# State-space scan by pairs of heads, and cross attention's small steps, placed between the chunks of weight units

## What is computed

```python
    xbc = jax.nn.silu(_depthwise_causal_conv(xbc, ssd_conv_w, ssd_conv_b))
    xs, bm, cm = jnp.split(xbc, [SSD_INNER, SSD_INNER + SSD_GROUPS * SSD_STATE], axis=-1)
...
    cb = jnp.einsum('bclgn,bcsgn->bgcls', Cc, Bc)
    y_diag = jnp.einsum('bgrcls,bcsgrp->bclgrp', cb[:, :, None] * Lmat, X)
    decay_states = jnp.exp(a_cs[..., -1:] - a_cs)
    states = jnp.einsum('bclgn,bgrcl,bclgrp->bcgrpn', Bc, decay_states, X)
...
    y_off = jnp.einsum('bclgn,bcgrpn,bgrcl->bclgrp', Cc, prev_states, jnp.exp(a_cs))
...
    y = (y + ssd_D.astype(jnp.float32)[:, None] * xh).astype(x.dtype).reshape(b, s, SSD_INNER)
    yg = (y * jax.nn.silu(z)).reshape(b, s, SSD_GROUPS, SSD_INNER // SSD_GROUPS)
    y = _rmsnorm(yg, ssd_norm_g.reshape(SSD_GROUPS, SSD_INNER // SSD_GROUPS), SUBLN_EPS)
    ssd_out = y.reshape(b, s, SSD_INNER) @ w_branch_ssd
    g_attn, g_ssd = jnp.split(jax.nn.sigmoid(gate_logits + b_gate), N_BRANCH, axis=-1)
    mixed = (g_attn * attn_out + g_ssd * ssd_out) @ w_mix_out
...
    sc = jnp.einsum('bqhd,bkhd->bhqk', qx, kx).astype(jnp.float32) * (XA_HEAD_DIM ** -0.5)
    p = jax.nn.softmax(sc, axis=-1).astype(vx.dtype)
```

## Time and profile before

| | |
|---|---|
| median of three runs | 2845.43 us |
| profiled execution | 2849.17 us, span in the trace 2847.1 us |
| PE busy | 2652.6 us, 93% |
| PE weight loads, beside the matmuls | 2131.6 us, 75% |
| DVE, ACT, POOL busy | 1302.4, 1068.2, 183.1 us |
| HBM read | 237.94 MB |
| scan stage, 40 units | from 1661.6 us |
| gated stage, 24 units | from 2026.8 us |
| next stage's first matmul | 2170.5 us |

### The profile page before, as it was taken

One profiled execution on the slowest core, in us unless ns is written; L12 is line 12 of the kernel. 1 busy time (PEld: TensorE's weight loads), 2 busy tenths in 40 slices (PEclk: granted clock), 3 DMA queues, 4 the chain that ended last, 5 costly groups with the idle time before them and its releaser, 6 DMA issues. The chain is left out here.

```text
span 2847.1 us, 33597 instructions
## 1 busy us (share of the span) xinstructions
PE 2652.6 (93%) x12052; PEld 2131.6 (75%) x12052; DVE 1302.4 (46%) x1758; ACT 1068.2 (38%) x1677; POOL 183.1 (6%) x114
## 2 busy tenths in 40 slices
PE   7998999999999999996999998889799799799997
PEld 5886777788888888884777776677587587588885
DVE  7544453454443344424344455666534533533333
ACT  5444453232222323323556434443423443332321
POOL 1000000010001000012000001101303200100000
PEclk9999999999999999998999999999899899899998
DMA  3212122233333333332222223222233122133332
GB/s 117 72 52 86 60 66 74 82 96 96 98 97 95 98 97 98 92 97 69 67 67 67 68 97 96 96 92 85 67 96 102 60 91 80 52 96 96 96 95 82
DMA packets 69471, 241.20 MB, mean 85 GB/s; under 512 B 7968, under 2 KB 8992, under 8 KB 69264
## 3 DMA queue, kind: packets, MB, share of 16 engines
q1 hardware_dynamic: 69392, 240.14, 26.7%
HBM read 237.94 MB, written 2.16 MB: 84 GB/s over the span
## 5 line engine op out<-in xcount | busy, mean ns | idle before, releaser
L193 PE MATMUL acc<-h_hi,w_hi 128*128 128x512 f32 x2128 | 856.3, 402 | 26.7 <-PEq L230 17.2
L166 DVE TENSOR_TENSOR w_lo<-w_raw,w_hi 128x1024 fp32r<-128x1024 f32 (+1 forms) x422 | 513.9, 1218 | 791.7 <-ACT w_hi L155 791.5
L155 ACT ACTIVATE w_hi<-w_raw 128x1024 fp32r<-128x1024 f32 (+1 forms) x422 | 441.5, 1046 | 1093.9 <-PE acc L195 1092.6
L194 PE MATMUL acc<-h_lo,w_hi 128*128 128x512 f32 x2128 | 833.9, 392 | 0.0
L195 PE MATMUL acc<-h_hi,w_lo 128*128 128x512 f32 x2128 | 833.5, 392 | 0.0
L193 PEld LDWEIGHTS acc<-h_hi,w_hi 128*128 128x128 f32 x2128 | 402.8, 189 | 129.4 <-issue 40.9
L194 PEld LDWEIGHTS acc<-h_lo,w_hi 128*128 128x128 f32 x2128 | 403.2, 189 | 86.7 <-issue 6.7
L195 PEld LDWEIGHTS acc<-h_hi,w_lo 128*128 128x128 f32 x2128 | 402.6, 189 | 85.6
L193 PE MATMUL acc<-6_hid_hi,w_hi 128*128 128x512 f32 x352 | 136.9, 389 | 0.0
L194 PE MATMUL acc<-6_hid_lo,w_hi 128*128 128x512 f32 x352 | 136.9, 389 | 0.0
L195 PE MATMUL acc<-6_hid_hi,w_lo 128*128 128x512 f32 x352 | 136.9, 389 | 0.0
(11 more groups left out here) (436 smaller groups left out, 3505.0 us busy)
## 6 DMA issues: line engine op xcount, KB each, us to landing
w_raw<-in_w_gu SPq DMA_DIRECT2D x132, 512.0 KB, 3.5
w_raw<-in_w_down SPq DMA_DIRECT2D x48, 512.0 KB, 3.5
w_raw<-in_w_ssd SPq DMA_DIRECT2D x40, 512.0 KB, 3.5
w_raw<-in_w_swa SPq DMA_DIRECT2D x28, 512.0 KB, 3.5
w_raw<-in_w_gla SPq DMA_DIRECT2D x24, 512.0 KB, 3.5
w_raw<-in_w_da SPq DMA_DIRECT2D x24, 512.0 KB, 3.5
w_raw<-in_w_ssd_out SPq DMA_DIRECT2D x24, 512.0 KB, 3.5
w_raw<-in_w_xa SPq DMA_DIRECT2D x24, 512.0 KB, 3.6
```

The source lines that it names most:

```text
L155: c.nc.scalar.activation(c.w_hi[:, k % 2, 0:chunks * P], c.raw[:, k % 2, 0:chunks * P], ACT.Copy).then_inc(c.hi_done, 1)
L166: c.nc.vector.tensor_tensor(c.w_lo[:, k % 2, 0:chunks * P], c.raw[:, k % 2, 0:chunks * P], c.w_hi[:, k % 2, 0:chunks * P].bitcast(F32), AL ...
L193: pe.matmul(out, hi, x_hi[:, j, 0:cols], start=first, stop=False)
L194: pe.matmul(out, hi, x_lo[:, j, 0:cols], start=False, stop=False)
```

## The change

The scan stage becomes `scan_stage` with one stream of 48 units, without a loop: for each group B, C, then x and z of each pair in turn, and after the last group the eight gate units that stood in the gated stage. Every small step of a pair is done for that pair alone and placed between two chunks of a later unit: x's transposes and the states in the next x unit, the sum of squares, `po` and `pd` in the next z unit. The tap with the newest input and the bias is taken by ACT from PSUM (`Identity`) instead of by DVE. The decays of a pair are weighed in one instruction of 1024 columns. The gated stage becomes `values_stage` with 16 units; the split of `y_ssd` now stands in front of its first unit. In cross attention a head's score tiles go, two at a time, behind chunks 3 and 7 of the next head's first unit, its transposes behind chunks 1 and 5 of the fourth, its outputs behind chunk 1 of the fifth.

The core of the diff (left out: declarations, DMA order, the parts of `ssd_stage` that are removed and stand above; lines of a new function are shown without what they replace):

```diff
+            def score(n):
+                if n == 0:
+                    wait_evacuated(c, pe, i, 6 * j - 2)
+                    wait_evacuated(c, pe, i, 6 * j - 1)
+                att.score_tile(pe, g - 1, n, lambda m: [(q[:, before, e, :], k_[:, before, e, :]) for e in range(2)])
+            def scores_between(chunk):
+                if chunk in (3, 7):
+                    for n in (chunk // 2 - 1, chunk // 2):
+                        score(n)
+            def turns_between(chunk):
+                if chunk in (1, 5):
+                    for n in (chunk // 2, chunk // 2 + 1):
+                        att.transpose_tile(pe, g - 1, before, n)
+            def outputs():
+                att.outputs(pe, g - 1, lambda kt, e: v_tok[:, before, kt, e * P:(e + 1) * P])
+            def outputs_between(chunk):
+                if chunk == 1:
+                    outputs()
...
+            if not project:
+                for n in range(NT):
+                    score(n)
+                pe.wait_ge(v_done, g + 1)
+                att.transposes(pe, g - 1, before)
+                outputs()
+                return
+            multiply_tile(c, pe, i, 6 * j, 6 * j, mem, MEM, between=scores_between if attend else None)
+            for u in (1, 2):
+                multiply_tile(c, pe, i, 6 * j + u, 6 * j + u, mem, MEM)
             if attend:
                 pe.wait_ge(v_done, g + 1)
+            multiply_tile(c, pe, i, 6 * j + 3, 6 * j + 3, mem, MEM, between=turns_between if attend else None)
+            multiply_tile(c, pe, i, 6 * j + 4, 6 * j + 4, h, norm=None if attend else norm,
+                          between=outputs_between if attend else None)
...
             g = 2 * i + j
+            if attend:
+                att.maxima(dve, g - 1, (j - 1) % 2)
             if project:
                 for u in range(2):
                     split_lo(c, dve, i, 6 * j + u)
             if attend:
                 weights(g - 1, (j - 1) % 2)
             if project:
-                for u in (2, 3):
+                for u in (2, 3, 4):
                     split_lo(c, dve, i, 6 * j + u)
             if attend:
                 finish(g - 1)
             if project:
-                split_lo(c, dve, i, 6 * j + 4)
-                att.maxima(dve, g, j % 2)
                 split_lo(c, dve, i, 6 * j + 5)
         heads_of(dve, head)
...
+def scan_units(a):
+    order = [(n, g) for g in range(SSD_GROUPS) for n in ("b", "c", *(f"{n}{j}" for j in range(GH // 2) for n in "xz"))]
+    index = {"b": 0, "c": 1, **{f"x{j}": 2 + j for j in range(4)}, **{f"z{j}": 6 + j for j in range(4)}}
+    units = [(KC, lambda i, n=n, g=g: a["w_ssd"][g, index[n]]) for n, g in order]
+    units += [(KC, lambda i, g=g: a["w_ssd_out"][g, 0]) for g in range(KC)]
...
+        def turn_x(p):
+            i, j = divmod(p, GP)
+            pe.wait_ge(silued, 6 * i + 3 + j)
+            if p > 0:
+                pe.wait_ge(x_dt, p)
             for t in range(NT):
+                mm = pe.transpose(px[:, at(t)], xs[:, j % 2, at(t)], c.ident[:])
+            mm.then_inc(turned, 1)
+        def make_states(p):
+            pe.wait_ge(x_end, p + 1)
+            if p > 0:
+                pe.wait_ge(states, 5 * p)
             for t in range(3):
+                mm = pe.matmul(pst[:, at(t)], b_tok[:, t, :], xend[:, t, :], start=True, stop=True)
+            mm.then_inc(state_raw, 1)
+        def outputs(p):
+            pe.wait_ge(states, 5 * (p + 1))
+            if p > 0:
+                pe.wait_ge(moved_done, p)
+                pe.wait_ge(skip_done, p)
+            for t in range(1, NT):
+                mm = pe.matmul(po[:, at(t)], state[:, t - 1, :], c_[:, at(t)], start=True, stop=True)
+            mm.then_inc(off_done, 1)
+            pe.wait_ge(weighed, p + 1)
+            for h in range(2):
+                for t in range(NT):
+                    mm = pe.matmul(pd[64 * h:64 * h + 64, at(t)], xdt[:, t, SSD_P * h:SSD_P * (h + 1)],
+                                   m[:, h, at(t)], start=True, stop=True)
+            mm.then_inc(diag_done, 1)
...
+        for i in range(G):
+            p = GP * i
+            if i == 0:
+                unit("b", i)
+                unit("c", i)
+                unit("x0", i, between({3: [(turn_b, i)]}))
+            else:
+                unit("b", i, between({0: [(turn_x, p - 1)], 6: [(make_states, p - 1)]}))
+                unit("c", i, between({5: [(mean_square, p - 2), (outputs, p - 1)]}))
+                unit("x0", i, between({3: [(turn_b, i)]}))
+            unit("z0", i, between({5: [(c_by_b, i)]}))
+            unit("x1", i, between({0: [(turn_x, p)], 6: [(make_states, p)]}))
+            unit("z1", i, between({5: [(mean_square, p - 1), (outputs, p)] if i > 0 else [(outputs, p)]}))
+            for j in range(2, GP):
+                unit(f"x{j}", i, between({0: [(turn_x, p + j - 1)], 6: [(make_states, p + j - 1)]}))
+                unit(f"z{j}", i, between({5: [(mean_square, p + j - 2), (outputs, p + j - 1)]}))
+        p = GP * G
+        unit("gate", 0, between({0: [(turn_x, p - 1)], 6: [(make_states, p - 1)]}))
+        unit("gate", 1, between({5: [(mean_square, p - 2), (outputs, p - 1)]}))
+        unit("gate", 2)
+        unit("gate", 3, between({0: [(mean_square, p - 1)]}))
+        for g in range(4, KC):
+            unit("gate", g)
...
+        def take(name, i):
+            n, k = CONV.index(name), places[name, i]
+            wait_tile(c, act, 0, k)
+            if 6 * i + n >= 2:
+                act.wait_ge(convolved, 6 * i + n - 1)
+            act.activation(u[:, n % 2, 3:], c.acc[k % 2][:], ACT.Copy).then_inc(taken, 1)
+            act.activation(conv[:, n % 2, :], c.acc[k % 2][:], ACT.Identity, scale=small("ssd_conv_w_2", 24 * i + 18 + n),
+                           bias=small("ssd_conv_b_2", 6 * i + n)).then_inc(c.acc_free[k % 2], 1)
+            split_hi(c, act, 0, k)
...
+        def z_silu(j, i):
+            k, p = places[f"z{j}", i], GP * i + j
+            wait_tile(c, act, 0, k)
+            if p >= 2:
+                act.wait_ge(y_done, p - 1)
+            act.activation(zs[:, j % 2, :], c.acc[k % 2][:], ACT.Silu).then_inc(c.acc_free[k % 2], 1)
+            wait_evacuated(c, act, 0, k)
+            act.sem_inc(z_done, 1)
+            split_hi(c, act, 0, k)
...
+        act.wait_ge(padded, 1)
+        for i in range(G):
+            act.preload_act_table(ACT.Silu)
+            take("b", i)
+            silu("b", i)
+            take("c", i)
+            silu("c", i)
+            act.wait_ge(b_turned, i + 1)
+            act.activation(b_tok[:], pb[:], ACT.Copy).then_inc(b_tok_done, 1)
+            if i > 0:
+                square(GP * i - 1)
             for j in range(GP):
+                act.preload_act_table(ACT.Silu)
+                take(f"x{j}", i)
+                silu(f"x{j}", i)
+                z_silu(j, i)
+                act.preload_act_table_set(EXP_LN_SET)
+                decays(GP * i + j)
+                if j > 0:
+                    square(GP * i + j - 1)
+                if j == 1 and i > 0:
+                    root(i - 1)
+        act.preload_act_table(ACT.Sigmoid)
+        gate(0)
+        gate(1)
+        square(GP * G - 1)
+        gate(2)
+        act.preload_act_table_set(EXP_LN_SET)
+        root(G - 1)
+        act.preload_act_table(ACT.Sigmoid)
+        for g in range(3, KC):
+            gate(g)
...
+        def scale_x(p):
+            i, j = divmod(p, GP)
+            dve.wait_ge(turned, p + 1)
+            if p > 0:
+                dve.wait_ge(diag_done, p)
+            dve.tensor_tensor(by_head(xdt[:]), by_head(px[:].rearrange("p (t l) -> p t l", t=NT)), rate(i, j, DT, NT),
+                              ALU.mult).then_inc(x_dt, 1)
+            dve.wait_ge(x_dt, p + 1)
+            if p > 0:
+                dve.wait_ge(state_raw, p)
+            dve.tensor_tensor(by_head(xend[:]), by_head(xdt[:, 0:3]), rate(i, j, TO_END, 3), ALU.mult).then_inc(x_end, 1)
...
+        def finish(p):
+            i, j = divmod(p, GP)
+            dve.wait_ge(off_done, p + 1)
+            dve.wait_ge(pair_decayed, p + 1)
+            if p > 0:
+                dve.wait_ge(joined, p)
+            dve.tensor_tensor(moved[:, P:], po[:, P:], pair_decay[:, P:], ALU.mult).then_inc(moved_done, 1)
+            dve.wait_ge(diag_done, p + 1)
+            dve.wait_ge(silued, 6 * i + 3 + j)
+            dve.scalar_tensor_tensor(y_out[:, p, :], xs[:, j % 2, :], small("ssd_D_2", p), pd[:],
+                                     ALU.mult, ALU.add).then_inc(skip_done, 1)
...
+        for i in range(G):
+            p = GP * i
+            low("b", i)
+            convolve("b", i)
+            if i > 0:
+                finish(p - 1)
+            low("c", i)
+            convolve("c", i)
             for j in range(GP):
+                low(f"x{j}", i)
+                convolve(f"x{j}", i)
+                cut(p + j)
+                if j > 0:
```

(54 more changed lines are left out.)

432 lines of the change are left out of this document (187 added, 245 removed).

## The result

| kernel | us, median | range of its runs | ratio to before | 95% interval |
|---|---|---|---|---|
| before | 2844.9 | 2843.5 to 2853.5 | 1 | |
| changed | 2795.8 | 2795.2 to 2800.9 | 0.9825 | 0.9802 to 0.9848 |

The changed kernel takes 49 us less, 1.75%. The forecast of 2804 us was right in sign and in range (2786 to 2826), and 8 us too high.

A forecast was written before the change was run, and what follows sets the result against it. TensorE (PE), busy 93% of the span, was taken as the bound, so gains must come from its idle or lower-clock time. Profiled 2849.17 - 36.6 - 4.5 = 2808 us, less 3.7 to the median: 2804 us, range 2786 to 2826.

The forecast's parts named there:

- head, group starts, port: Scan stage: half clock at its head 3.0 us, waits at four group starts 17, GpSimd and DVE sharing a port 6.
- PE's own work: Scan stage: small steps 5.0 us a pair, 80 for 16 pairs; with B and C steps and 48 units, 346.5 us.
- The group starts: Start of each scan group: PE waits 2.8 us for a late ACT-DVE chain, plus 1.4 for lower clock; 17 us in all.
- The shared port: Scan pairs: GpSimd steps now run beside DVE's low part of z and slow it; 6 us (0 to 22).
- this toll in every pair: Rival, scan pairs: GpSimd blocks a low part or tap each time, 22 us, or lower clock, 27; 2826 to 2831; chance 0.17.
- Does a pair fit: Middle scan pairs: other engines fit within PE's 15.9 us, 0.7 us left at the tightest point, so no added cost.
- doesn't do what it says: Rival, scan stage: steps between chunks block PE like whole units, 43 us eat the gain; 2846; chance 0.03.
- ACT's ring: Scan pairs: ACT's cycle of work for one pair takes 14.1 us of PE's 15.9.
- the slower rival: Scan pairs: ACT's ring becomes the bound; saving used up at 18.5 us, 2869 us at 20; chance 0.03.
- Cross attention: Head's small steps spread two by two, new wait 1.2 us at third memory unit; 4.5 us saved (0 to 7).
- The sum: Whole kernel: 36.6 us saved in scan and values, 4.5 in cross attention; profiled 2808, forecast median 2804 us.
- nothing waits: Rival, scan stage: no waits at group starts and the port costs nothing; 2787 us; chance 0.20.

The follow-up runs named there:

- e9: Changed kernel with ACT reading one tile ahead at group starts, no repeated silu load, and cross attention's first weight split between exponentials: 2774.5 us, ratio 0.9739.
- e3: Changed kernel without the repeated load of silu's table ahead of each group's first x: 2786.0 us, ratio 0.9780 to before.
- e5: Changed kernel with ACT reading one tile ahead at group starts, repeated silu load left out, B transposes one chunk later: 2778.0 us, ratio 0.9752 to before.
- e7: Changed kernel with two more unused GpSimd products in each pair, started when z's silu is done: 2814.9 us, ratio 0.9882 to before.
- e10: Changed kernel with five more unused 512-column copies on ACT in each pair: 2820.7 us, ratio 0.9906 to before.
- e11: Changed kernel with eight more unused 512-column copies on ACT in each pair: 2838.7 us, ratio 0.9966 to before.
- e1: Kernel before with the new cross attention alone, old scan and gated stages: 2844.0 us, ratio 0.9989 (0.9979 to 1.0000) to before.

## Why the prediction came out as it did

The working on record, term by term, against the trace of the changed kernel. All are us.

| term | on record | measured | from |
|---|---|---|---|
| 48 units | 261.1 | 261.1 | 5.44 each, |
| small steps of 16 pairs | 80.0 | 72.2 | 15.39 from pair to pair, less 10.88 |
| B transposes, C by B | 5.4 | 4.7 | 0.36 and 0.81, four times |
| head, group starts, port | 26.0 | 20.7 | what is left of 358.7 |
| between the stages | 4.4 | 4.3 | 2020.0 to 2024.3 |
| values | 90.4 | 90.4 | 2024.3 to 2114.7 |
| exit | 5.0 | 4.5 | to 2119.2 |
| together | 472.3 | 457.9 | |

**PE's own work** was the largest miss, 7.8 us. I took 1.02 us for the eight `pd` passes of one head and doubled it for two. The 1.02 was right, for the wait of 0.32 us in the earlier trace rows stands in front of the row and not in it. Doubling it was wrong, because the passes of the second head do not wait for the first head's to end. The passes of one head start 0.11 us apart in both kernels; the second head's begin 0.49 us after the first head's, in each of the 16 pairs, and 0.49 + 1.02 are the 1.51 us measured. The table of stretches for the tile `pd` alone counts the passes at work (length; PE, PEld, DVE busy; clock, DMA, GB/s). First the changed kernel, ten passes in the middle third, then the eight passes of the earlier trace rows:

```profile
1875.64:1876.14 0.50, 0.49 (x5) 0.49 (x5) 0.00 (x0) 1.00 0.00 0
1876.14:1876.63 0.49, 0.49 (x10) 0.49 (x9) 0.00 (x0) 1.00 0.00 0
1876.63:1877.16 0.53, 0.53 (x7) 0.36 (x4) 0.00 (x0) 1.00 0.10 8
```

```profile
1745.80:1746.30 0.50, 0.49 (x5) 0.49 (x6) 0.15 (x1) 1.00 0.09 25
1746.30:1746.83 0.53, 0.53 (x6) 0.35 (x4) 0.53 (x1) 1.00 0.72 286
```

The matmuls of a head have 64 of PE's 128 columns (128*64 in the rows), and each head writes its own half of `pd`. In the kernel before each head's passes had a semaphore of their own to wait for, and the earlier trace rows show one head alone. That overlap is 0.53 us a pair, 8.5 us in all; the errors of the other small steps, some 0.1 us each, nearly cancel.

**The group starts** were right in place and cause, and somewhat too dear. On record: a wait of 2.6 us at four transposes, released by ACT's silu, 0.25 for a low part, 1.4 for the clock, together 17. Measured: four waits of 1.87 us and one of 1.1, 8.6 us, and the half clock for 3.4 us behind three of the four, 5.1 us: 13.7. e9, which has none of these waits, spends 16.7 us less from the first scan unit to the first value unit (346.3 against 363.0), of which 1.7 are a shorter half clock at the head of the stage. The diagnosis of the load was right, and e3 turned it into 10 us. What I had not said is that the chain is too late even without the load, since silu of c and two more steps stand ahead of the reads of x0 (e5).

**The shared port** was right as a risk and its size too large: 6 on record, under 1 in the trace, where one wait of 0.17 us for `x_to_end` is all that PE shows of it. In the changed kernel 8 of 47 low parts of the stage were hit, with up to 1.06 us more each, three of them in the first group, for which the sum had none; no one of the 72 taps was (all between 0.74 and 0.75 us). On the timeline of the second pair GpSimd and then DVE have

```profile
1724.30 1.29 POOL L2954 TENSOR_TENSOR y_ssd<-y_ssd,13_z_silu 128x512 f32<-128x512 f32 x1
```

```profile
1724.38 2.29 DVE L166 TENSOR_TENSOR w_lo<-w_raw,w_hi 128x1024 fp32r<-128x1024 f32 x1 [1.32 <-ACT w_hi L155]
```

so that the low part lasts longer by about what was left of GpSimd's product, and e7 did the same to taps. The Trainium skill (SBUF — State Buffer, Who interferes with whom) calls the port pair that VectorE and GpSimd share "an exclusive lock", and says, of VectorE's 2-port modes, that the engine that comes second "**fully blocks** (not throttle)". These rows and e7's agree with it for instructions with two inputs in SBUF, and the taps that I had left open follow the rule too. In the changed kernel it cost almost nothing, because most of these low parts stand where the chain to the states has some 0.9 us of room (1.06 us more at 1724.38 left a wait of 0.17), or because GpSimd, for which nobody waits, is the one that is blocked (2.05 instead of 1.01 us at 1802.80). The rival that priced this toll in every pair at 22 us was wrong on this kernel. That e7 came to 20 us is no confirmation of it, since most of that fell on the group starts.

**Does a pair fit** and **doesn't do what it says**: a pair cost PE's time alone, as said. ACT's ring of 14.1 us and its price beyond PE's period were right (e10, e11), so the slower rival was correctly drawn and correctly far away. By e10 and e11 it would have come true at about 4.8 us more in each pair.

**Cross attention**: 4.5 us on record, 4.0 in the trace, 2.9 (0 to 6) by e1, with the wait at the third memory unit at 1.0 instead of 1.2. The 1.9 us lost behind it were not foreseen; 1.6 of them are the lower clock in the first unit of the output projection, whose cause stays open.

**The sum**: 2804, less 14.3 in the scan, plus 0.5 in cross attention, plus 1.9 behind it, less 0.7 elsewhere, and plus 4.1 because I took 3.7 us off for the distance between the profiled execution and the median, while the profiled execution of after lies 0.4 below its own. That makes 2795.5, against 2795.8 measured. In the frame of the profiled executions the sum was 12.7 us too high (2808 against 2795.35); the subtraction brought the forecast nearer by luck. The 508.9 us from which the saving was counted held about 4 us of scatter (505.0 for the same code in e1), so most of what I subtracted stood in the stages that the change replaces. The case "nothing waits" (2787) did not come: the waits at the group starts were there, and PE's own work was cheaper instead. e9 shows what that case is worth when it is made to happen, 2774.5.

## What to carry to other kernels

Laying the small steps of one item beside the weight units of the next, with what came along in the same stage, was worth 45 to 47 us, and whether they stand inside a unit or at its edge hardly mattered; what mattered next was the first item of each group, where a chain over two engines (6.6 us and more a tile) is longer than PE's unit (5.44 us) and nothing older is left to overlap. There, have the evacuating engine read the next tile before it waits for the result of the last and before any step that is not urgent, and look for table loads of a set that is in place: the two were 17 us together. Before you multiply the time of a block of small matmuls, ask whether two such blocks can run side by side, and count its time from first start to next start; doubling the block of one head was the largest error of this forecast.

## What the runs showed of the hardware

- `pd` passes of two heads, 64 columns wide each, ran beside one another: eight took 1.02 us, sixteen 1.51, at the full clock in both cases.
- GpSimd and DVE, each with two inputs in SBUF, did not slow one another evenly; the later instruction became longer by about what was left of the earlier (0.75 to 1.04 us in e7, where 0.95 to 1.18 was left). A low part of 1.23 us took up to 2.35, a tap of 0.75 up to 1.67 (e7), GpSimd's 384 columns 2.05 instead of 1.01. DVE's product that reads PSUM (x times dt) kept its 0.68 us beside GpSimd.
- A load of a table whose set is in place took the full 1283 ns when other work stood between it and the load before; of two more written directly behind it the trace has none. Who left them out is not shown.
- In the changed kernel the waits of 1.87 us were followed by the lower clock (1.2 GHz) in the first three groups, for some 3.4 us, and not in the fourth: the groups' stretches have 0.94, 0.98, 0.98 and 1.00. Behind the waits of 0.75 us in e3 the chunks kept their pace.
- The same code of cross attention took 151.4 and 156.3 us in two kernels that differ only ahead of it, 2.7 us of it by longer matmuls at a mean clock of 0.92 instead of 0.94. The first unit behind it took 5.6 or 7.2 us, behind the same wait of 2.0 us.
